# Projecting q and k from x before it is normalised, with GpSimd scaling h for the LRU and v

## The chip, the cores and the metric

The kernel runs on one core of a Trainium2 chip. The metric is the device time of one execution in microseconds, the median of several runs. Everything is float32; each weight matrix is read once from HBM, 1 MB at a time.

## The reference, cut to what matters

```python
h = rms_norm(x, mix_norm_g)                 # x: 256 tokens x 1024
proj = h @ w_in                             # 1024 x 2560
xr, yg, q, k, v = jnp.split(proj, splits, axis=-1)
xr = causal_depthwise_conv(xr, ...)
y_lru = rg_lru(xr, ...) * gelu(yg)
q = rms_norm(q.reshape(.., HEADS, HEAD_DIM), q_norm_g)   # 8 heads of 64
k = rms_norm(k.reshape(.., HEADS, HEAD_DIM), k_norm_g)
y_attn = moba_attention(q, k, v)            # causal attention over one block of 256
x = x + concat(rms_norm(y_lru), rms_norm(y_attn)) @ w_out
hf = rms_norm(x, ffn_norm_g)
up = causal_depthwise_conv(hf @ w_up, ...)  # 1024 x 5632
gate, val = jnp.split(up, 2, axis=-1)
x = x + (gelu(gate) * val) @ w_down         # 2816 x 1024
```

`rms_norm(x, g)` is `x * rsqrt(mean(x*x) + 1e-6) * g` over the last axis. As q and k are normalised again in each head, a factor that is the same for a whole token cancels there, but for the 1e-6: with x instead of the normalised x, the head's root needs 1e-6 * (mean(x*x) + 1e-6) in its place.

## The kernel before, in words

Each float32 product is made of three products of a rounded type: an operand is split in a high part (the value rounded) and a low part (the value less the high part), and high x high, high x low and low x high are added in PSUM (`three`, lines 953 to 959).

**The stream of weights.** The weights come as units of 128 x 1024, two units to a transfer `raw[n]` of 1 MB, six transfers in flight, in the order of their use: units 0 to 3 are w_in's columns of q, 4 to 7 k, 8 to 11 the LRU's input, 12 to 15 its gate branch, 16 to 19 v, 20 to 27 w_out, then the FFN's. SyncE issues the two halves of x (128 tokens each, lines 268 and 269), then unit 0 (line 272), unit 1 (line 273), `raw[1]` to `raw[5]` (line 275), and from then on a transfer whenever VectorE has finished with a buffer. ScalarE copies a unit's high part to a ring of six (`hi(u)`, line 336), VectorE makes its low part (`lo(u)`, line 627), and TensorE waits for `lo_done` before it uses the unit. Unit 0 is split by halves, the first half by VectorE alone (lines 669 and 664), the second half's high part by ScalarE (line 376).

**The start.** TensorE does 14 products of a matrix of ones (`warm_up(WARM_UP)`, line 1008). ScalarE and VectorE meanwhile sum the squares of x (lines 347, 361, 651), take the root and the reciprocal (358, 365, 641) and scale x to `x_norm` (354, 645), for the first 128 tokens and then the second. TensorE transposes `x_norm` (line 1014: eight transposes for each half); ScalarE reads each chunk of 128 channels from PSUM, times the gain, into h's high part (`h_part`, line 370), and VectorE makes its low part (line 659).

**Up to the attention.** TensorE's list (from line 1058) is: q's units 0 to 3 (`rows_unit`, 12 products each, tokens in PSUM's rows), k's 4 to 7, the LRU's 8 and 9 (`cols_unit`, channels in the rows, 24 products each), the transposes of q and k (line 1020), which wait for `qk_norm` (line 1064), units 10 and 11 with the scores of the first heads between them, and so on. For the q and k norms ScalarE squares an accumulator (line 392), VectorE sums it by heads (690), ScalarE takes the root (396), VectorE the reciprocal (695) and the scaling (697). Each engine works through its list in order, which is written out by hand. ScalarE's and VectorE's lists have `hi` and `lo` of a unit at fixed places: h_part(0), unit 0's half, h_part(1), h_part(2), unit 1, h_part(3 to 5), unit 2, h_part(6), h_part(7), units 3 to 8, the q norms, units 9 to 11, the k norms, units 12 and 13.

GpSimd's list is short: constants, the parameters' transfer (line 306), the table of distances (lines 313 and 316), eight small fills, and, once VectorE has made unit 3's low part (`lo_done` 4), the transfer of the LRU's gate weights (line 326). It computes nothing after that.

The tiles `decay` and `gate_i` hold `x_norm` at the start, and `tanh_a` a square; all are free until the LRU's gates.

Of the kernel before, what the change touches and what calls it, by code (L numbers as in the profile page):

```python
# [30 lines left out]
P = 128  # L31
D_MODEL = 1024
SEQ = 256
# [65 lines left out]
def build_layer(nc, x, stream, params, gates, out):  # L99
    with ExitStack() as ctx:  # L100
# [34 lines left out]
        small = sb("small", [P, 208])  # L135
# [19 lines left out]
        x_norm = [flat(decay), flat(gate_i)]  # L155
        sq_tok = flat(p_T)[:, 2560:3072]
# [12 lines left out]
        x_part, x_mean = small[:, 206:207], small[:, 207:208]  # L169
# [14 lines left out]
        warm, x_normed = sem("warm"), [sem(f"x_normed{m}") for m in range(TT)]  # L184
        first_hi, first_lo = sem("first_hi"), sem("first_lo")
        x_sq, x_sq_1 = sem("x_sq"), sem("x_sq_1")
        own_hi, q_scale_done, f_added = sem("own_hi"), sem("q_scale_done"), sem("f_added")
        x_rms_done, x_rec = sem("x_rms_done"), sem("x_rec")
# [41 lines left out]
        Q_ACC, K_ACC, X_ACC = bank[0:2], bank[2:4], bank[4:8]  # L230
        Y_ACC, V_ACC = bank[2:4], bank[4:6]
# [34 lines left out]
        def _(sp):  # L266
# [5 lines left out]
            sp.dma_start(raw[0][:, 0:UNIT], stream[0, :, 0:UNIT]).then_inc(first_landed, 16)  # L272
# [54 lines left out]


        @block.scalar
        def _(act):  # L330
# [11 lines left out]

            act.wait_ge(consts, 1)
            act.activation(warm_out, eps, ACT.Sqrt).then_inc(warm, 1)

            act.wait_ge(x_landed[0], 16)
            act.activation(flat(ygate), x_tok[:, 0, :], ACT.Square, accum_out=x_ss[:, 0:1]).then_inc(x_sq, 1)
            def x_root(m):
                act.activation(x_rms[:, m:m + 1], x_ss[:, m:m + 1], ACT.Sqrt, bias=eps,
                               scale=1.0 / D_MODEL).then_inc(x_rms_done, 1)  # L350

            def x_scale(m):
                act.wait_ge(x_rec, m + 1)
                act.activation(x_norm[m][:, 0:F_CUT], x_tok[:, m, 0:F_CUT], ACT.Copy,
                               scale=x_rstd[:, m:m + 1]).then_inc(x_normed[m], 1)

            act.wait_ge(x_sq, 1)
            act.activation(x_rms[:, 0:1], x_ss[:, 0:1], ACT.Sqrt, bias=eps, scale=1.0 / D_MODEL).then_inc(x_rms_done, 1)

            act.wait_ge(x_landed[1], 16)  # L360
            act.activation(flat(ygate)[:, 0:512], x_tok[:, 1, 512:1024], ACT.Square, accum_out=x_ss[:, 1:2]).then_inc(x_sq, 1)
            x_scale(0)
            act.wait_ge(x_sq, 2)
            act.wait_ge(x_sq_1, 1)
            act.activation(x_rms[:, 1:2], x_ss[:, 1:2], ACT.Sqrt, bias=x_mean, scale=1.0 / D_MODEL).then_inc(x_rms_done, 1)
            x_scale(1)

            def h_part(kc):
# [927 lines left out]
```

## Time and profile before

| | |
|---|---|
| median of 3 runs | 304.53 us (304.36 to 304.56) |
| the profiled execution | 304.15 us |
| its span | 302.4 us |
| TensorE busy | 295.6 us, 98% of the span |
| VectorE busy | 242.1 us, 80% |
| ScalarE busy | 200.7 us, 66% |
| GpSimd busy | 3.9 us, 1% |
| granted TensorE clock | 1.0 of full speed |

The profile is one execution. Its span runs from the first to the last instruction; the profiled execution's own time is 1.75 us longer. PE is TensorE, PEld its weight loads, ACT ScalarE, DVE VectorE, POOL GpSimd, SPq SyncE's queue. Busy time of an engine that is not the bottleneck may be free; an engine that is busy 98% sets the time wherever it does not wait.

### The profile page before, as it was taken

The numbers are of one execution on the slowest core, as the hardware profiler recorded it, in microseconds if no ns is written. First come the engines' busy times: TensorE is split into PE (matmuls) and PEld (weight loads), VectorE is DVE, ScalarE is ACT, GpSimd is POOL, SyncE is SP. The second block draws the span as 40 slices with busy tenths as digits, with TensorE's granted clock in tenths as the row PEclk, the third lists the DMA queues.
The fourth block names the chain that finished last, engine by engine and source line by source line (L and its number), as shares of the span: only waits on it lengthen the run. The fifth ranks groups of instructions, "written<-read, shape, count | busy, mean of one in ns | idle before, by whom it ended". The sixth has DMA issues, their size and how long they took to land.

```text
span 302.4 us, 4942 instructions
## 1 busy us (share of the span) xinstructions
PE 295.6 (98%) x1656; PEld 255.2 (84%) x1656; DVE 242.1 (80%) x432; ACT 200.7 (66%) x370; POOL 3.9 (1%) x21
## 2 busy tenths in 40 slices
PE   8999999999999999899999999999999999999995
PEld 8788998898988788788888888888888888888884
DVE  2998597798799767899878888887788888787764
ACT  6874598997756376887666667666666666766540
POOL 4000000000000000000000000000000000000000
PEclk9999999999999999999999999999999999999999
DMA  7999843034406701566554445373645545300003
GB/s 247 427 420 424 369 146 139 2 139 139 141 8 261 288 2 18 185 238 252 207 203 148 172 159 230 139 277 139 256 160 170 202 148 180 132 0 0 0 0 139
DMA packets 7983, 52.22 MB, mean 173 GB/s; under 512 B 896, under 2 KB 896, under 8 KB 2080
## 3 DMA queue, kind: packets, MB, share of 16 engines
q1 hardware_dynamic: 7776, 51.38, 45.5%
q0 software_dynamic: 192, 0.64, 0.6%
q8 instruction: 9, 0.15, 0.2%
q14 instruction: 6, 0.05, 0.1%
HBM read 50.98 MB, written 1.05 MB: 172 GB/s over the span
## 4 chain that ended last, share of the span: by engine, by line
PE 91%; DVE 3%; DMA 2%; ACT 1%; issue 1%; SPq 0%; ACTq 0%
PE bank L1201 27%; PE bank L955 15%; PE bank L956 15%; PE bank L959 15%; PE bank L1203 13%; DMA raw<-in_stream_dram 2%; PE bank L1031 1%; DVE x_tok L947 1%; PE bank L1044 1%; DVE w_lo L627 1%; PE bank L1150 1%; PE bank L1149 1%; PE bank L1020 1%; PE bank L1143 1%; PE bank L1051 1%
## 5 line engine op out<-in xcount | busy, mean ns | idle before, releaser
L1201 PE MATMUL bank<-h_both,w_hi 128*128 128x512 f32 x352 | 125.1, 398 | 1.5 <-DVE w_lo L627 1.2
L627 DVE TENSOR_TENSOR w_lo<-raw,w_hi 128x1024 fp32r<-128x1024 f32 x93 | 111.0, 1221 | 10.0 <-ACT w_hi L336 9.0
L1203 PE MATMUL bank<-h_both,w_lo 128*128 128x256 f32 x352 | 98.7, 280 | 0.0
L336 ACT ACTIVATE w_hi<-raw 128x1024 fp32r<-128x1024 f32 x87 | 88.9, 1053 | 6.1 <-PE bank L959 4.6
L1201 PEld LDWEIGHTS bank<-h_both,w_hi 128*128 128x128 f32 x352 | 66.1, 188 | 18.0 <-issue 2.0
L1203 PEld LDWEIGHTS bank<-h_both,w_lo 128*128 128x128 f32 x352 | 66.4, 189 | 0.7
L554 ACT ACTIVATE tanh_a<-bank 128x256 f32<-128x256 f32 x44 | 16.8, 382 | 45.9 <-PE bank L1203 45.9
L956 PE MATMUL bank<-w_lo,act_hi 128*128 128x512 f32 x88 | 34.5, 392 | 0.0
L955 PE MATMUL bank<-w_hi,act_hi 128*128 128x512 f32 x88 | 34.5, 392 | 0.0
L959 PE MATMUL bank<-w_hi,act_lo 128*128 128x512 f32 x88 | 34.2, 389 | 0.0
L885 DVE TENSOR_TENSOR ygate<-bank,tanh_a 128x256 f32<-128x256 f32 x44 | 18.5, 421 | 13.2 <-ACT tanh_a L554 13.2
L562 ACT ACTIVATE xc<-ygate,par 128x256 f32<-128x256 f32 x44 | 26.2, 595 | 2.0 <-DVE ygate L885 2.0
L896 DVE SCALAR_TENSOR_TENSOR xc<-ygate,par,xc 128x254 f32<-128x254 f32 x44 | 21.3, 483 | 5.1 <-DVE xc L892 0.2
L892 DVE SCALAR_TENSOR_TENSOR xc<-ygate,par,xc 128x255 f32<-128x255 f32 x44 | 21.1, 481 | 3.4 <-ACT xc L562 3.1
L955 PEld LDWEIGHTS bank<-w_hi,act_hi 128*128 128x128 f32 x88 | 16.5, 188 | 3.9
L959 PEld LDWEIGHTS bank<-w_hi,act_lo 128*128 128x128 f32 x88 | 16.5, 188 | 3.6
L955 PE MATMUL bank<-w_hi,h_both 128*128 128x512 f32 x48 | 19.0, 396 | 0.6 <-DVE h_both L659 0.6
L956 PEld LDWEIGHTS bank<-w_lo,act_hi 128*128 128x128 f32 x88 | 16.5, 188 | 2.7
L959 PE MATMUL bank<-w_hi,h_both 128*128 128x512 f32 x48 | 18.7, 390 | 0.0
L956 PE MATMUL bank<-w_lo,h_both 128*128 128x512 f32 x48 | 18.7, 389 | 0.0
L955 PE MATMUL bank<-h_both,w_hi 128*128 128x256 f32 x64 | 18.7, 292 | 0.0
L956 PE MATMUL bank<-h_both,w_hi 128*128 128x256 f32 x64 | 18.1, 283 | 0.0
(162 smaller groups left out, 388.3 us busy)
## 6 DMA issues: line engine op xcount, KB each, us to landing
raw<-in_stream_dram SPq DMA_DIRECT2D x46, 1024.0 KB, 4.8
x_tok<-in_x_dram SPq DMA_DIRECT2D x2, 512.0 KB, 3.7
raw<-in_stream_dram SPq DMA_DIRECT2D x2, 512.0 KB, 7.0
out_dram<-x_tok SPq DMA_DIRECT2D x4, 256.0 KB, 2.1
p_T<-in_gates_dram POOLq DMA_DIRECT2D x1, 512.0 KB, 8.7
par<-in_params_dram POOLq DMA_DIRECT2D x1, 117.0 KB, 4.9
```

Of the source, the lines that this page charges most:

```text
L336: act.activation(w_hi[u % RING][:, :], raw_unit(u), ACT.Copy).then_inc(hi_done, 1)
L554: act.activation(cross[which][s % 2], up_bank(s, which)[:, SEQ:2 * SEQ], ACT.Copy).then_inc(cross_out, 1)
L562: act.activation((conv_g, conv_v)[which][s % 2], joined[which][s % 2], ACT.Identity, bias=par[:, bass.ds(col + FFN_B, 1)], scale=par[:, ba ...
L627: dve.tensor_tensor(w_lo[u % RING][:, :], raw_unit(u), w_hi[u % RING][:, :].bitcast(F32), ALU.subtract).then_inc(lo_done, 1)
L885: dve.tensor_tensor(joined[which][s % 2], up_bank(s, which)[:, 0:SEQ], cross[which][s % 2], ALU.add).then_inc((joined_g, joined_v)[which], 1)
L892: dve.scalar_tensor_tensor(acc[:, 1:SEQ], joined[which][s % 2][:, 0:SEQ - 1], par[:, bass.ds(col + (FFN_W + 2 * STEPS), 1)], acc[:, 1:SEQ] ...
L896: dve.scalar_tensor_tensor(acc[:, 2:SEQ], joined[which][s % 2][:, 0:SEQ - 2], par[:, bass.ds(col + FFN_W, 1)], acc[:, 2:SEQ], ALU.mult, AL ...
L955: pe.matmul(acc, lhs_hi, rhs_hi, start=first, stop=False)
L956: pe.matmul(acc, lhs_hi, rhs_lo, start=False, stop=False)
L959: return pe.matmul(acc, lhs_lo, rhs_hi, start=False, stop=last)
L1201: pe.matmul(acc[:, :], whi[:, kc, :], h_both[:, kc, :, :].rearrange("p b t -> p (b t)"), start=kc == 0, stop=False)
L1203: ins = pe.matmul(acc[:, 0:SEQ], wlo[:, kc, :], h_hi[:, kc, :], start=False, stop=kc == KC - 1)
```

## The change

Three things are changed.

1. TensorE transposes x as it lands. `h_part` makes from it `q_hi` and `q_lo` (x times the gain, not normalised; they use the tiles `mix_hi` and `mix_lo`), and q's and k's units multiply those. The heads' roots get `qk_bias`, a number for each token, so that one root instruction becomes two (one for each 128 tokens).
2. The mean squares of x are summed by ScalarE alone, the first half at once, the second after h_part(7) and before `hi(3)`. VectorE makes the means (`x_mean_squares`) ahead of `lo(3)`, and after it the reciprocal roots and two diagonal matrices (`x_diagonals`). After unit 2, TensorE multiplies ones by the diagonals: each token's factor stands then in all rows of a bank, and ScalarE copies it to `x_rows` after `hi(5)`. GpSimd adds `q_hi` and `q_lo` (eight instructions of 128 x 256) and multiplies by `x_rows` (eight more) into `h_norm`, in the tiles `decay` and `tanh_a`. ScalarE and VectorE split `h_norm` in `h_hi` and `h_lo`, after the q norms and around unit 9. The LRU's, its gate branch's and v's units use those; unit 8 waits for them chunk by chunk (`hn_lo`).
3. The transfer of unit 0 is issued by ScalarE, ahead of its first instruction, and not by SyncE.

```diff
@@ sync
-            sp.dma_start(raw[0][:, 0:UNIT], stream[0, :, 0:UNIT]).then_inc(first_landed, 16)
@@ gpsimd
+            pool.wait_ge(dist_done, TT + HEADS)
+            pool.wait_ge(hT_lo, KC)
+            for kc in range(KC):
+                pool.tensor_tensor(h_norm[kc], q_hi[:, kc, :].bitcast(F32), q_lo[:, kc, :].bitcast(F32),
+                                   ALU.add).then_inc(h_joined, 1)
+            pool.wait_ge(x_rows_done, 1)
+            for kc in range(KC):
+                pool.wait_ge(h_joined, kc + 1)
+                pool.tensor_tensor(h_norm[kc], h_norm[kc], x_rows[:, :], ALU.mult).then_inc(h_normed, 1)
@@ scalar
+            act.dma_start(raw[0][:, 0:UNIT], stream[0, :, 0:UNIT]).then_inc(first_landed, 16)
...
-            (squares, roots and x_scale of both halves)
+            x_square(0)
...
             for kc in (6, 7):
                 h_part(kc)
-            his(3, 4, 5, 6, 7, 8)
+            x_square(1)
+            his(3)
+            act.wait_ge(x_ms_done, 1)
+            act.activation(x_rms, x_ms, ACT.Sqrt).then_inc(x_rms_done, 1)
+            his(4, 5)
+            act.wait_ge(x_spread, 1)
+            act.activation(x_rows[:, :], X_ROWS, ACT.Copy).then_inc(x_rows_done, 1)
+            his(6, 7, 8)
...
+            act.wait_ge(qk_bias_done, 1)
             roots(0)
-            his(9, 10, 11)
+            for kc in range(4):
+                h_norm_hi(kc)
+            his(9)
+            for kc in range(4, KC):
+                h_norm_hi(kc)
+            his(10, 11)
@@ vector
-            (reciprocals, squares and x_scale of both halves)
...
             for kc in (6, 7):
                 h_part(kc)
+            x_mean_squares()
             los(3)
+            x_diagonals()
...
             head_norms(0, Q_ACC)
-            los(9, 10, 11)
+            for kc in range(4):
+                h_norm_lo(kc)
+            los(9)
+            for kc in range(4, KC):
+                h_norm_lo(kc)
+            los(10, 11)
@@ tensor
             for m in range(TT):
-                pe.wait_ge(x_normed[m], 2)
+                pe.wait_ge(x_landed[m], 16)
                 for kc in range(KC):
-                    ins = pe.transpose(x_at(kc)[...], x_norm[m][:, P * kc:P * (kc + 1)], ident[:, :])
+                    ins = pe.transpose(x_at(kc)[...], x_tok[:, m, P * kc:P * (kc + 1)], ident[:, :])
...
             for j in range(4):
-                rows_unit(U_Q + j, U_Q, Q_ACC, hT_lo)
+                rows_unit(U_Q + j, U_Q, Q_ACC, q_hi, q_lo, hT_lo)
+                if j == 2:
+                    pe.wait_ge(x_diag, TT)
+                    for m in range(TT):
+                        ins = pe.matmul(X_ROWS[:, P * m:P * (m + 1)], ones[:, :], diag[:, m, :], start=True, stop=True)
+                    ins.then_inc(x_spread, 1)
             for j in range(4):
-                rows_unit(U_K + j, U_K, K_ACC)
-            cols_unit(U_X, X_ACC[0][:, 0:SEQ])
+                rows_unit(U_K + j, U_K, K_ACC, q_hi, q_lo)
+            cols_unit(U_X, X_ACC[0][:, 0:SEQ], h_ready=hn_lo)
```

The new functions, as far as they are not told above:

```python
def x_diagonals():                                    # VectorE
    dve.wait_ge(x_rms_done, 1)
    link(dve.reciprocal(x_rstd, x_rms))
    dve.wait_ge(consts, 2)
    for m in range(TT):
        dve.tensor_scalar(diag[:, m, :], ident[:, :], x_rstd[:, m:m + 1], None, ALU.mult).then_inc(x_diag, 1)

def h_norm_hi(kc):                                    # ScalarE
    act.wait_ge(h_normed, kc + 1)
    act.activation(h_hi[:, kc, :], h_norm[kc], ACT.Copy).then_inc(hn_hi, 1)

def h_norm_lo(kc):                                    # VectorE
    dve.wait_ge(hn_hi, kc + 1)
    dve.tensor_tensor(h_lo[:, kc, :], h_norm[kc], h_hi[:, kc, :].bitcast(F32), ALU.subtract).then_inc(hn_lo, 1)
```

## Rows read from the trace of the kernel before

**Rows 1.** The page, busy us (share of the span) xinstructions.

```profile
PE 295.6 (98%) x1656; PEld 255.2 (84%) x1656; DVE 242.1 (80%) x432; ACT 200.7 (66%) x370; POOL 3.9 (1%) x21
```

**Rows 2.** Chain of waits to the first weight product: start us, us, what.

```profile
1.75 6.20 DMA raw<-in_stream_dram
...
9.12 0.41 DVE h_both L659
...
9.67 0.47 PE bank L955
```

**Rows 3.** Timeline of TensorE's weight loads: start us, us, engine line op.

```profile
1.08 6.03 PEld L1005 LDWEIGHTS bank<-ones 128*128 128x128 f32 x28 [1.08 <-POOL ones L304]
7.14 0.86 PEld L1014 LDWEIGHTS bank<-ident,decay 128*128 128x128 f32 x8
7.96 0.91 PEld L1014 LDWEIGHTS bank<-ident,gate_i 128*128 128x128 f32 x8
```

**Rows 4.** Timeline of ScalarE from 4 to 17 us.

```profile
4.11 1.06 ACT L347 ACTIVATE ygate<-x_tok 128x1024 f32<-128x1024 f32 x1 [1.79 <-DMA x_tok<-in_x_dram]
...
5.29 0.29 ACT L358 ACTIVATE small<-small 128x1 f32<-128x1 f32 x1
...
8.44 0.47 ACT L370 ACTIVATE h_both<-bank,par 128x256 fp32r<-128x256 f32 x1 [0.64 <-PE bank L1014]
...
12.46 1.06 ACT L336 ACTIVATE w_hi<-raw 128x1024 fp32r<-128x1024 f32 x1 [0.27 <-DMA raw<-in_stream_dram]
...
14.14 2.95 ACT L336 ACTIVATE w_hi<-raw 128x1024 fp32r<-128x1024 f32 x3
```

**Rows 5.** Timeline of VectorE from 6 to 37 us.

```profile
6.48 0.54 DVE L645 TENSOR_SCALAR decay<-x_tok,small 128x640 f32<-128x640 f32 x1
...
11.14 1.23 DVE L627 TENSOR_TENSOR w_lo<-raw,w_hi 128x1024 fp32r<-128x1024 f32 x1 [0.20 <-ACT w_hi L336]
...
15.49 1.22 DVE L627 TENSOR_TENSOR w_lo<-raw,w_hi 128x1024 fp32r<-128x1024 f32 x1
...
16.75 5.76 DVE L627 TENSOR_TENSOR w_lo<-raw,w_hi 128x1024 fp32r<-128x1024 f32 x5
...
32.42 0.69 DVE L690 TENSOR_REDUCE small<-p_T 128x8 f32<-128x512 f32 x1 [2.54 <-ACT p_T L392]
...
35.18 1.29 DVE L697 TENSOR_TENSOR qk_tok<-bank,small 128x512 f32<-128x512 f32 x2
```

**Rows 6.** Timelines of TensorE: unit 3's first product, the q/k transposes, line 1114.

```profile
17.99 0.39 PE L955 MATMUL bank<-w_hi,h_both 128*128 128x512 f32 x1
...
37.35 1.91 PE L1020 MATMUL bank<-ident,qk_tok 128*128 128x128 f32 x16
...
82.58 0.66 PE L1114 MATMUL bank<-diag,ones 128*128 128x128 f32 x4
83.08 0.33 PE L1149 MATMUL bank<-v_tok,p_T 128*128 128x64 f32 x2
```

**Rows 7.** Groups of VectorE: xcount | busy us, mean ns | idle before.

```profile
L636 DVE TENSOR_SCALAR diag<-ident,small 128x128 f32<-128x128 f32 x2 | 0.6, 288 | 0.1
```

**Rows 8.** Timeline of GpSimd, 3 to 18 us.

```profile
3.56 0.40 POOL L316 TENSOR_SCALAR_AFFINE_SELECT neg_dist<-neg_dist 128x256 f32<-128x256 f32 x1
4.02 1.14 POOL L322 MEMSET small<- 64x1 f32 x8
17.01 0.59 POOL L326 DMA_DIRECT2D p_T<-in_gates_dram  x1 [11.85 <-DVE w_lo L627]
```

**Rows 9.** Groups of ScalarE and VectorE with SBUF operands of 128x256.

```profile
L574 ACT ACTIVATE act_hi<-gate_i 128x256 fp32r<-128x256 f32 x22 | 8.9, 403 | 1.4 <-DVE gate_i L905 1.4
L910 DVE TENSOR_TENSOR act_lo<-gate_i,act_hi 128x256 fp32r<-128x256 f32 x22 | 9.2, 419 | 0.5 <-ACT act_hi L574 0.5
```

**Rows 10.** DMA issues, KB each, median us from issue to landing.

```profile
x_tok<-in_x_dram SPq DMA_DIRECT2D x2, 512.0 KB, 3.7
raw<-in_stream_dram SPq DMA_DIRECT2D x2, 512.0 KB, 7.0
```

More of the change, by code:

```diff
@@ L155, in build_layer @@
         x_norm = [flat(decay), flat(gate_i)]
+        q_hi, q_lo = mix_hi, mix_lo
+        h_norm = [(decay, tanh_a)[kc // LC][:, kc % LC, :] for kc in range(KC)]
         sq_tok = flat(p_T)[:, 2560:3072]
@@ L183, in build_layer @@
         dist_done = sem("dist_done")
-        warm, x_normed = sem("warm"), [sem(f"x_normed{m}") for m in range(TT)]
+        warm = sem("warm")
+        x_ms_done, qk_bias_done, x_diag, x_spread, x_rows_done = (
+            sem("x_ms_done"), sem("qk_bias_done"), sem("x_diag"), sem("x_spread"), sem("x_rows_done"))
+        h_joined, h_normed, hn_hi, hn_lo = sem("h_joined"), sem("h_normed"), sem("hn_hi"), sem("hn_lo")
         first_hi, first_lo = sem("first_hi"), sem("first_lo")
-        x_sq, x_sq_1 = sem("x_sq"), sem("x_sq_1")
+        x_sq = sem("x_sq")
         own_hi, q_scale_done, f_added = sem("own_hi"), sem("q_scale_done"), sem("f_added")
-        x_rms_done, x_rec = sem("x_rms_done"), sem("x_rec")
+        x_rms_done = sem("x_rms_done")
         xT, hT_hi, hT_lo = sem("xT"), sem("hT_hi"), sem("hT_lo")
@@ L230, in build_layer @@
         Q_ACC, K_ACC, X_ACC = bank[0:2], bank[2:4], bank[4:8]
+        X_ROWS = bank[6][:, 0:SEQ]
         Y_ACC, V_ACC = bank[2:4], bank[4:6]
@@ new lines, in x_diagonals @@
+            def x_diagonals():
+                dve.wait_ge(x_rms_done, 1)
+                link(dve.reciprocal(x_rstd, x_rms))
+                dve.wait_ge(consts, 2)
+                for m in range(TT):
+                    dve.tensor_scalar(diag[:, m, :], ident[:, :], x_rstd[:, m:m + 1], None, ALU.mult).then_inc(x_diag, 1)
+            def h_norm_lo(kc):
+                dve.wait_ge(hn_hi, kc + 1)
+                dve.tensor_tensor(h_lo[:, kc, :], h_norm[kc], h_hi[:, kc, :].bitcast(F32),
+                                  ALU.subtract).then_inc(hn_lo, 1)
@@ L657, in h_part @@
             def h_part(kc):
                 dve.wait_ge(hT_hi, kc + 1 if kc < 4 else kc + 2 - kc % 2)
-                dve.scalar_tensor_tensor(h_lo[:, kc, :], x_at(kc), par[:, MIX_G + kc:MIX_G + kc + 1],
-                                         h_hi[:, kc, :].bitcast(F32), ALU.mult, ALU.subtract).then_inc(hT_lo, 1)
+                dve.scalar_tensor_tensor(q_lo[:, kc, :], x_at(kc), par[:, MIX_G + kc:MIX_G + kc + 1],
+                                         q_hi[:, kc, :].bitcast(F32), ALU.mult, ALU.subtract).then_inc(hT_lo, 1)
@@ L989, in rows_unit @@
                         tok = slice(P * m, P * (m + 1))
-                        ins = three(banks[m][:, :], h_hi[:, kc, tok], h_lo[:, kc, tok],
+                        ins = three(banks[m][:, :], lhs_hi[:, kc, tok], lhs_lo[:, kc, tok],
                                     w_hi[u % RING][:, cols], w_lo[u % RING][:, cols], kc == 0, kc == KC - 1)
```

68 lines of the change are left out of this document (23 added, 45 removed).

## The prediction

> **What bounds the kernel now.** I read the page's busy times first: TensorE is busy 98% of the span [rows 1], so only time in which it waits, or products added to it, can move the end. The span is 302.4 us, the profiled execution 304.15 us (1.75 us around the span), the median of the runs 304.53 us. I work in differences on the span and add them to the median.
>
> The chain of waits at the start says what the first weight product waits for [rows 2]: the transfer of unit 0 (landed 7.95), what VectorE makes of it, then h's low part, and the product at 9.67. That reads as if weights and normalisation were both too late. The second view to read is the timeline of the engine at the end of that chain [rows 3]: TensorE's 14 warm-up products end at 7.11 and the transposes of x follow at 7.14 and 7.96 without a gap. x_norm[0] was ready at 7.02 (VectorE's share, 6.48 + 0.54 [rows 5]), so the warm-up, not the normalisation, releases the transposes. The third view is ScalarE's own timeline [rows 4]: from 8.44 it works without a gap until 12.19 and then waits 0.27 us for raw[1], whose two units are units 2 and 3. VectorE behind it makes unit 1's low part at 11.14 to 12.37 [rows 5], and TensorE starts unit 1 right then. So units 1 to 3 are paced by ScalarE's list and by raw[1] landing at about 12.42, after which TensorE runs without a gap: unit 3 starts at 17.99, the q/k transposes at 37.35 [rows 6].
>
> **The change part by part.**
>
> *No normalisation before the transposes.* Removed: about 2.5 us of ScalarE and 1.9 us of VectorE work between 5.3 and 7.8. All of it lay beside the warm-up products, whose count the diff leaves at 14. The transposes start at 7.14 as before and h_part(0) on ScalarE at 8.44 as before. Gain: 0 on this path; the most it could be is the 0.09 us between 7.02 and 7.11. x must now have landed by 7.14 and 7.96. x took a median 3.7 us from issue [rows 10] and ScalarE began on the first half at 4.11 [rows 4], so the second came near 5.4; cover 2.5 us or more.
>
> *First weights through ScalarE's queue.* They are issued at about 0.83 instead of 1.75. Both x halves then share the transfer engines with them. All three transfers were through by 7.95 [rows 2], in whatever order, and that is the worst for x's second half; midway between 5.4 and 7.95 is 6.7. Its transposes start at 7.96 [rows 3]: covered. ScalarE's issue (0.4 us) and its table load end before x lands at 4.11. Gain: the first half's cast and subtraction are no longer in front of h_lo(0), which waited for VectorE until 9.04. It could start at 8.44 + 0.47 + 0.03 = 8.94, so the first product comes 0.1 us earlier. Unit 1 still needs VectorE's subtraction at 11.14, which waited for ScalarE's copy [rows 5], and that copy's place behind h_part(2) is the same: the 0.1 us is given back at 12.4. If the issue stood behind the table load, at 2.1 us, all would be 0.35 us late. Neither end reaches unit 3 by more than that; I take 0.
>
> *The square of x's second half, moved.* It now stands on ScalarE between h_part(7) and hi(3). Before, hi(3) started at 14.14. The full square costs 1.18 us, start to next start (4.11 to 5.29 [rows 4]). hi(3) starts at 15.3 and ends at 16.37; VectorE's lo(3) runs 16.41 to 17.63 where it had started at 15.49 (+0.92). TensorE would have needed lo(3) at 17.99: covered by 0.36 us.
>
> *The new row products.* TensorE now waits after unit 2 for two diagonals that VectorE makes behind lo(3): a reciprocal (0.16 us and its wait) and two scalings of 0.29 us that overlap to about 0.5 [rows 7], done at 18.25 to 18.3. Unit 3's products, which need nothing of this, are queued behind: wait 0.3 us. The two f32 products cost 0.50 us, as the same pair at line 1114 shows (82.58 to 83.08 [rows 6]). Unit 3 starts at 18.8: **+0.8 us**. Ends: +0.4 if raw[1] lands 0.3 us or more earlier, since then only the products remain; +1.3 if the extra queue makes it land 0.5 us later.
>
> *GpSimd joins and scales h.* Its list has the gates' transfer ahead, which waited for lo(3) and was issued at 17.01, 0.59 us long [rows 8]; with lo(3) 0.92 us later, the first sum starts at about 18.3, not when q_lo is there at 15.6. Then 8 sums and 8 scalings of 128x256. No row shows GpSimd with two operands. One operand of this size took 0.40 us: lower end. Two read one after the other, 0.80 us: upper end. I take 0.6, nearer the row: 16 x 0.6 = 9.6, done at 27.9. By the Trainium skill (GPSIMD Engine Reference, Performance versus the Vector engine) 4497 ns for 2048 elements gives an estimate of about 0.6 us too. Unit 8 starts at 31.6 + 0.8 and takes the chunks one by one; ScalarE's eight copies (0.40 [rows 9]) have to follow. Cost 0 for TensorE up to about 0.75 us an instruction.
>
> *VectorE's list grows.* Added before the k norms, in start-to-start times: lo(3) late 0.92; reciprocal and diagonals 0.6; a second square root in the q round 0.2; eight low parts of h at 0.42 us less 0.08 overlap [rows 9], 2.7. Together 4.4 us. The head sums of k began at 32.42 after 2.54 us of idle time [rows 5], so lo(11) had ended at 29.88; it now ends at 34.3 and they begin 1.9 us later. With one more square root the k norms, which ended at 35.18 + 1.29 = 36.47, end at 38.5, and TensorE arrives at 37.35 + 0.8 = 38.15: **a new wait of 0.4 us** (0 if the 0.08 overlaps are larger; 1 if VectorE loses 0.6 us more).
>
> Sum: +0.8 + 0.4 = +1.2 us. Behind line 1064 TensorE is gapless again until long after, so nothing is given back: 304.15 + 1.2 = 305.35 for the profiled execution, and against the median **305.7 us** (own range 304.9 to 306.5).
>
> **The rivals.**
>
> *Port: VectorE and GpSimd hold each other up (+7.2, 311.7 us).* From 18.3 on, VectorE's list is subtractions of two SBUF operands of 1.22 us (five in a row from 16.75 [rows 5]) and the eight short ones, and GpSimd's 16 instructions lie beside them. If each must wait for the other's to end and they take turns, VectorE waits behind four of its five long subtractions and six of the following ones, ten times 0.6 = 6.0 us; it has no slack left, so TensorE gets all of it before the q/k transposes: 1.2 + 6.0. With 0.4 us it is 309.7, with 0.8 313.7. It decides as soon as VectorE loses over 0.4 us. For it: a VectorE without idle time in this stretch. Against it: nothing in this trace, since GpSimd computes only until 5.2 us [rows 8], when VectorE has no such instruction; no row bears on it.
> The Trainium skill (SBUF — State Buffer, Who interferes with whom) states exactly this mechanism: a VectorE instruction with two SBUF inputs contends with a GpSimd instruction that reads SBUF, whoever is first holding the ports for the whole instruction. By that rule this rival is the result; no run here shows it yet.
>
> *GpSimd is slow alone (+3.6, 308.1 us).* At 0.9 us an instruction, 16 x 0.15 us past the cover of 0.75 is 2.4 us more. For it: a two-operand form that no row shows. Against: 0.40 us for one operand.
>
> *Not slower (+0.4, 304.9 us, within the measurement).* raw[1] lands before 12.1, because the queue of x gives up 512 KB or a lower rate of the first transfers fills up. Then ScalarE's copy of unit 2 starts at 12.19, the diagonals are ready when unit 2 ends, and the k norms are just in time; left are 0.5 us of row products less 0.1 at the start. For it: the first weights took 6.2 us from issue [rows 2] and the 512 KB loads a median 7.0 [rows 10]. Against it: all bytes ahead of raw[1] are the same.
>
> *Faster (303.8 us).* If the warm-up's end is only modelled late and the transposes start at 6.7, with the stream 1 us earlier too, units 1 to 3 come 0.4 us or more earlier and outweigh the products. Against it: rows 3 show no gap.
>
> **How the numbers follow.** Forecast 0.40, port 0.27, GpSimd slow 0.08, not slower 0.17, faster 0.08. A measurement of this kernel tells about 0.2%, 0.6 us, from no change. Slower: 0.37 of the forecast's 0.40 plus 0.35, 0.72; same: 0.03 + 0.17, 0.20; faster 0.08. The range 304.2 to 312.2 leaves out the faster case and the port case with the longest instructions. The signs hold different weights, so the forecast's own range stands above.
>
> **What would show it.** First transposes at 7.1 and unit 1 at 12.4 as before (else the first two parts are wrong); a wait of TensorE for the diagonals and unit 3 near 18.8; subtractions of line 627 still 1.22 us apart by 1.14 beside GpSimd (the port rival stretches them or opens gaps to about 1.8); GpSimd done by 28; k norms near 38.5. A VectorE gap or stretch of over 0.5 us per instruction after 18.3 would make 305.7 wrong upward; raw[1] landing before 12.1, downward.

## The result and the profile after

The changed kernel takes 311.07 us (median of 4 runs, 310.95 to 312.63) against 304.5 us before; the ratio is 1.0228, 95% interval 1.0196 to 1.0261. That is slower by 6.6 us where 305.7 was forecast, and 0.6 us below the 311.7 that the port rival gave. The profiled execution took 310.95 us, its span is 309.2 us against 302.4. Executions more than 1.5% above the fastest of their kernel are left out of the times and ratios below: three of seven of the kernel with the results scaled (312.77 to 314.32 us, mean granted clock 0.978 to 0.984) and one of 12 of the kernel without GpSimd's work and with the queue back (593 us).

Busy time, from the page of the kernel after (columns as in [rows 1]):

```profile
PE 298.4 (96%) x1660; PEld 256.9 (83%) x1660; DVE 247.6 (80%) x438; ACT 202.8 (66%) x378; POOL 21.9 (7%) x37
```

GpSimd's 16 new instructions are 18.0 us of that, 1.1 us each, where the forecast had 0.6. TensorE has only four instructions more, but it waits. The waits of TensorE, us in total, times, longest:

```profile
PE bank L982 <- DVE h_both L674: 2.0, 2, 1.8
PE bank L1047 <- DVE qk_tok L719: 2.0, 1, 2.0
...
PE bank L1041 <- DMA x_tok<-in_x_dram: 0.3, 1, 0.3
```

The timeline of TensorE says where the loss arises. Shown are the transposes of x, the first product, unit 1, the row products, unit 3, unit 8's first and fifth chunk, and the q/k transposes:

```profile
6.84 1.04 PE L1041 MATMUL bank<-ident,x_tok 128*128 128x128 f32 x8
8.15 1.09 PE L1041 MATMUL bank<-ident,x_tok 128*128 128x128 f32 x8 [0.28 <-DMA x_tok<-in_x_dram]
9.72 0.47 PE L982 MATMUL bank<-w_hi,mix_hi 128*128 128x512 f32 x1 [0.48 <-DVE mix_lo L679]
...
12.57 0.50 PE L982 MATMUL bank<-w_hi,mix_hi 128*128 128x512 f32 x1
...
18.17 0.60 PE L1090 MATMUL bank<-diag,ones 128*128 128x128 f32 x4
18.53 0.48 PE L982 MATMUL bank<-w_hi,mix_hi 128*128 128x512 f32 x1
...
32.22 0.28 PE L982 MATMUL bank<-h_both,w_hi 128*128 128x256 f32 x1
...
35.60 0.39 PE L982 MATMUL bank<-h_both,w_hi 128*128 128x256 f32 x1 [1.78 <-DVE h_both L674]
...
44.12 1.09 PE L1047 MATMUL bank<-ident,qk_tok 128*128 128x128 f32 x8 [1.96 <-DVE qk_tok L719]
```

Up to unit 3 the change costs 0.54 us (18.53 against 17.99 [rows 6]). The q/k transposes start at 44.12 against 37.35 [rows 6]: 6.77 us, which is all of the loss (6.8 us on the span). Behind them nothing comes and nothing is given back. So the question is what made the k norms, the last thing the transposes wait for, end at 44.07 instead of 36.47 [rows 5]. Timeline of VectorE:

```profile
17.91 7.40 DVE L647 TENSOR_TENSOR w_lo<-raw,w_hi 128x1024 fp32r<-128x1024 f32 x5
...
30.57 0.68 DVE L674 TENSOR_TENSOR h_both<-decay,h_both 128x256 fp32r<-128x256 f32 x1 [0.20 <-ACT h_both L370]
...
37.56 2.36 DVE L647 TENSOR_TENSOR w_lo<-raw,w_hi 128x1024 fp32r<-128x1024 f32 x2 [0.48 <-ACT w_hi L352]
39.84 0.68 DVE L712 TENSOR_REDUCE small<-p_T 128x8 f32<-128x512 f32 x1
...
42.78 1.29 DVE L719 TENSOR_TENSOR qk_tok<-bank,small 128x512 f32<-128x512 f32 x2
```

The five subtractions in a row took 5.76 us before [rows 5] and take 7.40 now: VectorE lost 1.6 us there. Behind 30 us it has gaps, and they end with ScalarE. Timeline of ScalarE, the last copies of h and what stands behind them:

```profile
29.42 0.42 ACT L370 ACTIVATE h_both<-decay 128x256 fp32r<-128x256 f32 x1 [1.52 <-POOL decay L342]
...
35.30 0.42 ACT L370 ACTIVATE h_both<-tanh_a 128x256 fp32r<-128x256 f32 x1 [1.25 <-POOL tanh_a L342]
36.16 0.42 ACT L370 ACTIVATE h_both<-tanh_a 128x256 fp32r<-128x256 f32 x1 [0.45 <-POOL tanh_a L342]
36.49 1.99 ACT L352 ACTIVATE w_hi<-raw 128x1024 fp32r<-128x1024 f32 x2
```

And timeline of GpSimd, the new instructions in their four groups of four:

```profile
18.24 7.67 POOL L337 TENSOR_TENSOR decay<-mix_hi,mix_lo 128x256 f32<-128x256 f32 x4
25.87 2.82 POOL L337 TENSOR_TENSOR tanh_a<-mix_hi,mix_lo 128x256 f32<-128x256 f32 x4
28.65 3.19 POOL L342 TENSOR_TENSOR decay<-decay,x_rows 128x256 f32<-128x256 f32 x4
31.80 4.33 POOL L342 TENSOR_TENSOR tanh_a<-tanh_a,x_rows 128x256 f32<-128x256 f32 x4
```

The second group is the measure of GpSimd undisturbed: 2.82 us for four, 0.70 from start to start and 0.74 long each, while VectorE reduces p_T (one operand, in SBUF) and begins to scale q out of PSUM. The first group, beside the five subtractions, takes 7.67. The chain then reads: the end of GpSimd's last scaling (36.13), ScalarE's copy (36.16), the high parts of units 10 and 11 queued behind it (36.49), VectorE's low parts (37.56), the squares and sums of k (39.84), the roots, the k norms (44.07).

The turn-taking itself is seen in two single instructions. First VectorE, then GpSimd, from windows between 22.5 and 25 us:

```profile
21.87 1.76 DVE L647 TENSOR_TENSOR w_lo<-raw,w_hi 128x1024 fp32r<-128x1024 f32 x1
...
23.55 1.76 DVE L647 TENSOR_TENSOR w_lo<-raw,w_hi 128x1024 fp32r<-128x1024 f32 x1
```

```profile
22.51 1.72 POOL L337 TENSOR_TENSOR decay<-mix_hi,mix_lo 128x256 f32<-128x256 f32 x1
```

The first of these subtractions ends at 23.63. GpSimd's sum, issued at 22.51, ends 0.60 behind that, at 24.23, and the next subtraction ends 1.1 behind that. These times fit two engines of which neither is interrupted and the one that comes second waits for the whole of the other. A turn takes 1.68 us (1.14 + 0.54), so VectorE loses 0.54 per turn and GpSimd about 1.0. The turns begin late, though. The first sum, issued at 18.24, let two subtractions pass and took 2.63 us:

```profile
18.24 2.63 POOL L337 TENSOR_TENSOR decay<-mix_hi,mix_lo 128x256 f32<-128x256 f32 x1
```

Those first two subtractions were not stretched (1.22 us each), so VectorE lost three times 0.54, the 1.6 us.

One more thing stands between 37 and 41 us. The row of windows 38 to 39 us (PE busy, PEld, DVE, ACT, POOL, granted clock, DMA share, GB/s):

```profile
38.00:39.00 1.00, 1.00 (x7) 1.00 (x6) 1.00 (x2) 0.96 (x2) 0.00 (x0) 0.50 0.97 410
```

After the 1.78 us wait in unit 8 the granted clock is 0.50 (1.2 GHz) from 37.1 to 40.5 and the products are 0.21 apart instead of 0.12. Here that is hidden: the k norms end 2 us later still.

### The profile page after: what moved, and what is told of

It is laid out like the page before. It is cut to its first block, busy times and chain, and to the rows that moved or that the text cites. A ratio compares the mean times of both kernels' runs of the same rounds, so it can differ in the third digit from the quotient of the medians.

```text
span 309.2 us, 4984 instructions
## 1 busy us (share of the span) xinstructions
PE 298.4 (96%) x1660; PEld 256.9 (83%) x1660; DVE 247.6 (80%) x438; ACT 202.8 (66%) x378; POOL 21.9 (7%) x37
## 4 chain that ended last, share of the span: by engine, by line
PE 81%; issue 5%; POOL 5%; DVE 5%; ACT 2%; POOLq 0%; ACTq 0%
PE bank L1233 26%; PE bank L1235 13%; PE bank L982 12%; PE bank L983 12%; PE bank L986 12%; POOL decay L337 2%; PE bank L1058 1%; DVE w_lo L647 1%; POOL tanh_a L337 1%; DVE x_tok L974 1%; ACT p_T L533 1%; PE bank L1071 1%; DVE h_both L887 1%; POOL decay L342 1%; ACT w_hi L352 1%
## 5 line engine op out<-in xcount | busy, mean ns | idle before, releaser
L647 DVE TENSOR_TENSOR w_lo<-raw,w_hi 128x1024 fp32r<-128x1024 f32 x93 | 112.9, 1240 | 10.3 <-ACT w_hi L352 9.5
L1235 PE MATMUL bank<-h_both,w_lo 128*128 128x256 f32 x352 | 98.7, 280 | 0.0
L982 PE MATMUL bank<-w_hi,mix_hi 128*128 128x512 f32 (+1 forms) x72 | 26.9, 374 | 0.5 <-DVE mix_lo L679 0.5
L986 PE MATMUL bank<-w_hi,mix_lo 128*128 128x512 f32 (+1 forms) x72 | 26.4, 366 | 0.0
L983 PE MATMUL bank<-w_lo,mix_hi 128*128 128x512 f32 (+1 forms) x72 | 26.4, 366 | 0.0
L982 PE MATMUL bank<-h_both,w_hi 128*128 128x256 f32 x64 | 19.5, 305 | 2.0 <-DVE h_both L674 2.0
L986 PE MATMUL bank<-h_both,w_lo 128*128 128x256 f32 x64 | 18.8, 294 | 0.0
L983 PE MATMUL bank<-h_both,w_hi 128*128 128x256 f32 x64 | 18.8, 294 | 0.0
```

What stands on the lines that cost most here:

```text
L647: dve.tensor_tensor(w_lo[u % RING][:, :], raw_unit(u), w_hi[u % RING][:, :].bitcast(F32), ALU.subtract).then_inc(lo_done, 1)
L982: pe.matmul(acc, lhs_hi, rhs_hi, start=first, stop=False)
L983: pe.matmul(acc, lhs_hi, rhs_lo, start=False, stop=False)
L986: return pe.matmul(acc, lhs_lo, rhs_hi, start=False, stop=last)
L1235: ins = pe.matmul(acc[:, 0:SEQ], wlo[:, kc, :], h_hi[:, kc, :], start=False, stop=kc == KC - 1)
```

## The experiments

Two theories were put against each other. **Lateness:** TensorE loses because GpSimd's list ends late and the h chain stands in front of the k norms. **VectorE's loss:** TensorE loses what the subtractions lose. The kernel before was run again beside each, on the same chip. Its median was 304.62 us beside the kernel without GpSimd's work, the one with long fills, the one with one operand on GpSimd and the one with the traffic beside the kernel before; 304.98 us beside the ones with one operand on VectorE, with half the instructions, with the queue back in the kernel after and with the results scaled; and 304.87 us beside the other four.

### GpSimd's work taken out

```
-  pool.tensor_tensor(h_norm[kc], q_hi, q_lo, ALU.add) ... pool.tensor_tensor(h_norm[kc], h_norm[kc], x_rows, ALU.mult)
   h_norm_hi(kc):  act.activation(h_hi, q_hi, ACT.Copy)         # was h_norm[kc], with a wait for GpSimd
   h_norm_lo(kc):  dve.tensor_tensor(h_lo, q_hi, h_hi, ALU.subtract)
```

> The changed kernel without GpSimd's 16 instructions; ScalarE and VectorE split q_hi instead of the scaled h (so the LRU and v get a wrong factor; the work of all other engines is unchanged). Port theory (the two engines hold each other up at SBUF): line 647's five subtractions after unit 3 go back from 7.40 to 5.8 us, the k norms end near 38.5 instead of 44.07, time 305.0 to 305.7. GpSimd-is-slow theory: the same, since it leaves GpSimd out. If the loss came from something else (the row products, the longer lists of ScalarE and VectorE), the time stays above 308.

Measured: 305.09 us (305.07 to 305.21), ratio 1.0003 [0.9958, 1.0048]. VectorE's timeline:

```profile
18.08 5.76 DVE L639 TENSOR_TENSOR w_lo<-raw,w_hi 128x1024 fp32r<-128x1024 f32 x5
...
36.99 1.29 DVE L711 TENSOR_TENSOR qk_tok<-bank,small 128x512 f32<-128x512 f32 x2
```

Everything else of the change is still in (only the scaling of h is left out): the transposes of raw x, the squares moved, the diagonals, the row products, 16 more short instructions on ScalarE and VectorE, the queue. All that costs 0.5 us or less; GpSimd's 16 instructions cost 6.0.

### GpSimd busy, but only writing

```
-  pool.tensor_tensor(h_norm[kc], ...)                      # 16 of them
+  pool.memset(flat(decay if kc % 2 else tanh_a), 0.0)      # 16 fills of 128x1024, then of 128x656
```

Both read h as in the experiment above and keep all waits for GpSimd. First with 1024 columns:

> As the kernel without GpSimd's work, but GpSimd does 16 fills of 128x1024 in its place, which read nothing, and ScalarE's eight copies wait for the last eight. Port theory, with reading as what collides: GpSimd's fills keep one duration whether VectorE subtracts or not, line 647 stays at 1.14 us from start to start; the time is that of the kernel without GpSimd if a fill is under 0.75 us, more by 16 times the excess. Any-GpSimd-work theory: fills and subtractions stretch each other as in the changed kernel, over 308.

Then with 656 columns:

> As the kernel with 16 fills in place of GpSimd's sums and scalings (h is not scaled), but each fill of 656 columns instead of 1024, so about 0.64 us each and 0.70 apart: the pace of undisturbed two-operand instructions. Theory (lateness of GpSimd's list is the whole price; at this pace unit 8's cover hides it): GpSimd ends near 29.6 to 30.2, the k norms end near 38.3 to 38.8, and the time is 305.1 us (304.9 to 305.8), as without GpSimd. Rival (anything that puts the h chain in the lists behind GpSimd costs the k norms, whatever its pace): the k norms end near 40 and the time is 307 or more.

Measured: 310.74 us (310.59 to 310.78), ratio 1.0187 [1.0141, 1.0233], with 1024 columns, and 305.04 us (304.85 to 305.21), ratio 1.0010 [1.0001, 1.0019], with 656. The last fill of each, GpSimd's timeline, and of the kernel with the shorter ones VectorE's:

```profile
33.47 0.95 POOL L341 MEMSET decay<- 128x1024 f32 x1
```

```profile
28.83 0.65 POOL L341 MEMSET decay<- 128x656 f32 x1
```

```profile
17.96 5.76 DVE L647 TENSOR_TENSOR w_lo<-raw,w_hi 128x1024 fp32r<-128x1024 f32 x5
...
36.86 1.29 DVE L719 TENSOR_TENSOR qk_tok<-bank,small 128x512 f32<-128x512 f32 x2
```

Fills aren't held up, and hold nobody up: 1.01 and 0.70 us apart throughout, VectorE's five at 5.76. So here lateness stands alone. The long fills end at 34.42 and the k norms at 42.36; the short ones, at the pace of undisturbed two-operand instructions, end at 29.48 and cost nothing. That is the lateness theory with VectorE's loss excluded. The forecast's cover, by which GpSimd's instructions cost TensorE nothing up to 0.75 us each, is confirmed too: 16 x (1.01 - 0.75) = 4.2 us, and the k norms moved from 38.15 to 42.36.

The time moved by 5.7, not 4.2. TensorE's q/k transposes show the rest:

```profile
42.42 3.36 PE L1047 MATMUL bank<-ident,qk_tok 128*128 128x128 f32 x16 [3.54 <-DVE qk_tok L719]
```

The granted clock fell to 0.50 in that wait of 3.54 us, at 41.9, and stayed there until 45.3; the 16 transposes took 3.36 instead of 1.91 us [rows 6].

### What GpSimd reads

```
-  pool.tensor_tensor(h_norm[kc], q_hi, q_lo, ALU.add)      /  pool.tensor_tensor(h_norm[kc], h_norm[kc], x_rows, ALU.mult)
+  pool.tensor_scalar(h_norm[kc], q_hi, 1.0, None, ALU.mult) /  pool.tensor_scalar(h_norm[kc], h_norm[kc], 1.0, None, ALU.mult)
```

> The changed kernel with each of GpSimd's 16 instructions reading one operand of 128x256 (a product with 1.0) in place of two. Port theory: still stretched beside VectorE's subtractions, though GpSimd alone takes about 0.4: the five subtractions take 6.5 to 7.4 us, time 306 to 309. GpSimd-is-slow theory (two operands are slow on GpSimd itself): each takes 0.4 throughout, subtractions back to 5.8 us, time as without GpSimd, about 305.5.

Measured: 312.13 us (311.97 to 313.29), ratio 1.0241 [1.0192, 1.0290]. Timeline of GpSimd, first and second group, and of VectorE:

```profile
18.48 6.75 POOL L337 TENSOR_SCALAR decay<-mix_hi 128x256 f32<-128x256 f32 x4
25.20 3.29 POOL L337 TENSOR_SCALAR tanh_a<-mix_hi 128x256 f32<-128x256 f32 x4
```

```profile
18.15 6.37 DVE L646 TENSOR_TENSOR w_lo<-raw,w_hi 128x1024 fp32r<-128x1024 f32 x5
```

One operand less doesn't help. Such an instruction is held off as well (6.75 us for four), and undisturbed they are 0.82 us apart, more than the two-operand one's 0.70. Both theories had put it at 0.4 us, so both missed the time (306 to 309 and 305.5). VectorE was stretched too, but less: 6.37 us for its five, against 7.40 beside two-operand sums and 5.76 alone. So both forms of a reading GpSimd instruction take part, and the fills, which read nothing, don't.

### What VectorE reads

```
   lo(u):
+      if u in (4, 5, 6, 7, 8):
+          dve.tensor_scalar(w_lo, raw_unit(u), 2.0 ** -13, None, ALU.mult); return
```

> The kernel after, with VectorE's subtractions of units 4 to 8 replaced by a scaling of raw alone (one SBUF operand, same output tile; the low parts of these units are then not the right ones). GpSimd's 16 two-operand instructions stay. Theory (what holds GpSimd off is that VectorE reads two SBUF operands, not that it is busy): GpSimd's sums take 0.74 us from the first, all 16 end at 29.6 to 30.5 instead of 36.1, the k norms end near 38.5 and the time is 305.0 to 305.6 us. Rival (any VectorE instruction that reads SBUF holds it off while it runs): the sums take 0.9 to 1.5 us, GpSimd ends at 32 or later and the time is over 307.

Measured: 310.05 us (308.53 to 311.08), ratio 1.0174 [1.0136, 1.0211]. Timeline of GpSimd and, second, VectorE:

```profile
17.68 1.74 POOL L332 DMA_DIRECT2D p_T<-in_gates_dram  x1 [12.48 <-DVE w_lo L650]
19.49 3.73 POOL L337 TENSOR_TENSOR decay<-mix_hi,mix_lo 128x256 f32<-128x256 f32 x4
...
23.19 1.19 POOL L337 TENSOR_TENSOR tanh_a<-mix_hi,mix_lo 128x256 f32<-128x256 f32 x1
```

```profile
18.01 1.29 DVE L648 TENSOR_SCALAR w_lo<-raw 128x1024 fp32r<-128x1024 f32 x2
20.30 3.48 DVE L648 TENSOR_SCALAR w_lo<-raw 128x1024 fp32r<-128x1024 f32 x3 [1.00 <-ACT w_hi L352]
...
40.41 1.29 DVE L722 TENSOR_TENSOR qk_tok<-bank,small 128x512 f32<-128x512 f32 x2
```

The theory fell. The rival holds for this instruction: the sums that met a scaling took 1.19 us, the three scalings from 20.30 took 3.48 us where two alone take 1.29, and even the issue of the gates' transfer took 1.74 instead of 0.59 [rows 8], until the two scalings at 18.01 were through. It doesn't hold for any VectorE instruction that reads SBUF, as the expectation put it: in the kernel after the sum of p_T over the heads, which reads 128x512 from SBUF, ran from 26.63 to 27.32 beside sums of 0.74 us. The scalings are shorter, so GpSimd ended at 33.75, not 36.13, and the k norms at 41.70, not 44.07: the same 2.4 us. What was wrong in the expectation is that it freed GpSimd: 30.5 at the latest. That the issue of a transfer is held up is read from one row only, and it is not the whole of the same mechanism: in the kernel after the same issue began at 17.58 and met a subtraction at 17.91, 0.33 us later as here, and took 0.59.

### The same traffic beside the kernel before

```
   # kernel before
+  for n in range(16):
+      pool.tensor_tensor(scratch, neg_dist[:, 0:SEQ], neg_dist[:, P:P + SEQ], ALU.add)   # nobody waits for it
+      pool.wait_ge(loads_done, n + 1)
```

> The kernel before, with 16 GpSimd sums of 128x256 added behind the gates' transfer (from about 17.6 us), for which no engine waits. Port theory: the five subtractions from 16.75 take about 7.4 us instead of 5.76, the sums take about 1.9 us beside them and 0.7 when VectorE is idle; TensorE loses at most 0.3 us, since VectorE had 2.5 us of idle time before the k norms: 304.5 to 304.9. GpSimd-is-slow theory: subtractions as before, sums of one length, 304.5.

Measured: 305.11 us (304.60 to 305.30), ratio 1.0000 [0.9954, 1.0046]. The first sum, GpSimd's timeline, and the five subtractions beside it, VectorE's:

```profile
18.18 5.44 POOL L331 TENSOR_TENSOR scratch<-neg_dist 128x256 f32<-128x256 f32 x1
```

```profile
17.25 5.77 DVE L633 TENSOR_TENSOR w_lo<-raw,w_hi 128x1024 fp32r<-128x1024 f32 x5
...
26.89 4.57 DVE L633 TENSOR_TENSOR w_lo<-raw,w_hi 128x1024 fp32r<-128x1024 f32 x3
```

With nobody waiting for GpSimd the traffic costs TensorE nothing that can be measured, though the later subtractions are stretched as in the kernel after (4.57 us for three, against 3.49 in the kernel before, from 26.39). The five in a row were not, where 7.4 us was expected: GpSimd's first sum stood through all of them, 5.44 us, and VectorE lost nothing. In the kernel after the first sum stood through two of them and then the two engines alternated. Who gets the next turn is thus not fixed; why the first sum got none here is open. The sums here read other tiles and each waits for the one before it, and neither was tried alone.

### Half the instructions

```
-  8 sums, then 8 scalings of the sum
+  8 x pool.tensor_tensor(h_norm[kc], q_hi, x_rows, ALU.mult)
```

> The kernel after with GpSimd's eight sums left out, so that it scales the high part of h alone: eight two-operand instructions instead of 16. Theory (one GpSimd instruction gets through per VectorE subtraction, 1.7 us apart, and what counts is when the list ends): it starts at 19.2 when x_rows is there, gets four through until VectorE's subtractions end at 25.3, the rest at 0.74, and ends near 28.5, ahead of what the copies of h need; the k norms end at 38.3 to 39 and the time is 305.1 to 306.0 us. VectorE still loses 1.0 to 1.6 us in its five subtractions, which are then seen not to matter. Rival (what VectorE loses is what TensorE loses): the k norms end 1 to 1.6 us later than without GpSimd, at 39.3 to 39.9, and the time is 306.1 to 306.7.

Measured: 306.65 us (306.46 to 306.86), ratio 1.0054 [1.0038, 1.0070]. VectorE's timeline:

```profile
17.87 7.40 DVE L643 TENSOR_TENSOR w_lo<-raw,w_hi 128x1024 fp32r<-128x1024 f32 x5
...
38.42 1.29 DVE L715 TENSOR_TENSOR qk_tok<-bank,small 128x512 f32<-128x512 f32 x2
```

GpSimd ended at 28.65 as expected, in good time. The k norms still ended at 39.71, 1.6 us later than with the short fills, and that is the 1.6 us that the five subtractions lost (7.40 against 5.76): here the rival theory is the right one, and it is what my rival in the prediction described. Both mechanisms exist. With GpSimd in time TensorE pays VectorE's loss, 1.6; with 16 instructions GpSimd's lateness is the longer path and covers it.

### The order of the lists

```
   his(9, 10, 11)                     # ahead of the eight h_norm_hi instead of between and behind them
   for kc in range(KC): h_norm_hi(kc)
   # and los(9, 10, 11) ahead of the eight h_norm_lo
```

> The kernel after, with the high and low parts of units 9, 10 and 11 put ahead of ScalarE's copies and VectorE's subtractions of h; GpSimd's 16 instructions stay. Theory (GpSimd's instructions are held to one per VectorE subtraction, and the k norms are late because they stand behind the h chain in both lists): hi(9..11) no longer wait for GpSimd, so the k norms wait only for eight subtractions of h behind GpSimd's end at about 36; they end near 41.2 instead of 44.1 and the time is about 308.2 us. Rival (the k norms are late because VectorE and TensorE themselves are slowed by GpSimd's traffic, whatever the order): 311 us as the kernel after. A second rival, that the order is right and the h part is needed early by unit 8: unit 8 waits over 3 us and the time is above 311.

Measured: 311.10 us (310.42 to 311.53), ratio 1.0203 [1.0183, 1.0222]: no change, and my 308.2 missed. TensorE's timeline at unit 8, and GpSimd's last group:

```profile
35.56 0.55 PE L976 MATMUL bank<-h_both,w_hi 128*128 128x256 f32 x1 [3.15 <-DVE h_both L671]
```

```profile
33.44 4.30 POOL L342 TENSOR_TENSOR tanh_a<-tanh_a,x_rows 128x256 f32<-128x256 f32 x4
```

Two things were left out of the expectation. The three subtractions now lie beside GpSimd's scalings, so its list ends at 37.74, 1.6 us later. And the first low part of h comes behind them: unit 8 waits 3.15 us, and the granted clock is 0.50 from 35.3 to 42.1 us. The second rival that the expectation named came true, as far as the wait goes. The k norms ended at 43.50, and TensorE reached the q/k transposes later still, at 44.62, without a wait. Order moves the wait from one place to the other; it doesn't remove it.

### The queue of the first weights

Alone on the kernel before, where x is normalised ahead of the transposes:

```
-  sp.dma_start(raw[0][:, 0:UNIT], ...)
+  act.dma_start(raw[0][:, 0:UNIT], ...)
```

> The kernel before, with only unit 0's transfer issued by ScalarE instead of SyncE. Theory (x then lands at about 8.2 instead of 5.4, and here x is normalised before it is transposed): x_norm[1] near 10.1, the first product near 11.6 instead of 9.7, about 1.9 us that TensorE can't give back: 306.5 us. Rival (the sixteen engines' rate is shared but x is small, or the warm-up hides it): first product within 0.3 of 9.7 and 304.5 us.

Taken back in the kernel after, and in the one without GpSimd's work:

> The kernel after with unit 0's transfer back on SyncE's queue. Theory (the start of the kernel lies ahead of GpSimd's lateness, which sets the k norms by itself): x lands 2 us earlier, the transposes of x no longer wait, the q/k transposes stay at 44.1 and the time is 311.0 us (310.8 to 311.5). Rival (the first units set GpSimd's start, so the loss moves with them): the time is 310.5 or less, or 311.7 or more where the first weights land later.

> The kernel without GpSimd's sums and scalings (h is not scaled), with unit 0's transfer back on SyncE's queue. Theory (x lands 2.3 us later through the second queue, and of that only some 0.2 to 0.3 us reaches TensorE, where the transposes wait for x): the wait for x goes, unit 3 starts 0.2 to 0.3 us earlier, and the time is 304.8 us against 305.1. Rival (the queue gives the stream an earlier first unit, which is what keeps this kernel so near the one before): the first product comes later than 9.9 and the time is 305.3 or more.

Measured: alone 307.51 us (307.41 to 308.67), ratio 1.0102 [1.0083, 1.0120]; taken back in the kernel after 312.96 us (311.50 to 313.86), ratio 1.0267 [1.0228, 1.0306]; taken back without GpSimd 305.42 us (304.75 to 307.15), ratio 1.0019 [0.9998, 1.0039]. TensorE's transposes in the first of them, then the first product in the second:

```profile
9.63 1.37 PE L1014 MATMUL bank<-ident,decay 128*128 128x128 f32 x8 [2.43 <-DVE decay L645]
```

```profile
10.76 0.47 PE L982 MATMUL bank<-w_hi,mix_hi 128*128 128x512 f32 x1 [1.78 <-DVE mix_lo L679]
```

The move has two sides. x takes 6.0 us from issue to landing instead of 3.7 [rows 10]; where x must be squared, rooted and scaled first, the transposes wait 2.43 us, the granted clock is 0.50 from 10.3 to 13.7 us, and the kernel loses 2.6 us (I had expected 2). The changed kernel doesn't have that step in front and waits 0.3 us. On the other side unit 0 landed by 6.5 us in every profile with the move in which VectorE stood waiting for it (6.25 in the kernel after), and without the move at 8.8 to 9.1 in three profiles and at 7.95 in that of the kernel before, whose first product at 9.67 [rows 2] is thus an early one. With unit 0 late, lo(3) ends 0.6 us later, GpSimd starts at 18.82 instead of 18.24 and the k norms end at 44.66 instead of 44.07. So the start is not hidden behind GpSimd, as my theory had it; it is the start of GpSimd's path. The two profiled executions, both at a mean clock of 0.994, are 0.55 us apart (311.50 and 310.95); the rest of the 1.9 us between the medians goes with a lower clock, 0.989 in two of the four executions. In the kernel without GpSimd the difference is within what can be told; the 304.8 us that the theory expected was not reached, and the first product came at 10.47, as its rival had it.

### The scaling put on the results

```
   q_hi, q_lo = h_hi, h_lo                                   # one split of h for all units, never scaled
+  dve.tensor_tensor(X_ACC[c], X_ACC[c], x_rows, ALU.mult)   # 4, in PSUM; and 4 halves of Y_ACC
   act.activation(v_tok[:, m, :], V_ACC[m], ACT.Copy, scale=x_rstd[:, m])
```

> The change without GpSimd: h is not scaled at all; VectorE scales the accumulators of X and Y by x_rows in PSUM, and ScalarE's copy of V takes 1/rms as its scale, so the whole result is computed. Theory (TensorE pays only the four row products, 0.4 to 0.5 us, and the six scalings of 128x256, about 0.4 us each, lie beside it): k norms end near 37 and the time is 304.9 to 305.2 us, no faster than before, since the transposes of x start when the warm-up ends in either. Rival (the scalings stand between the convolution and what TensorE next waits for): 306 us or more. Second rival (with eight subtractions of h gone, units and norms come early enough that it beats the kernel before): 304.2 or less.

Measured: 307.93 us (307.88 to 308.07 in four executions), ratio 1.0094 [1.0059, 1.0130]. Waits of TensorE:

```profile
PE bank L1177 <- ACT v_tok L498: 1.3, 1, 1.3
...
PE bank L1080 <- DVE xc L729: 1.0, 1, 1.0
```

The k norms end at 37.35, earlier than in any other version of the change, and the price comes later: TensorE waits 1.0 us for the convolution, in front of which the scalings now stand in VectorE's list, and 1.3 for v's copy. Which of these each scaling causes was not separated. (The profile is of an execution of 314.32 us, whose granted clock was 0.50 from 84.0 to 97.7 us; only what lies before that is read from it, the wait for v's copy at 82.4 us as the last.) The first rival was right, and my 304.9 to 305.2 missed. No version beat the kernel before.

## Why the prediction was right and wrong

**One rule ties the runs.** In five kernels the k norms end 7.9 us after GpSimd's last instruction, whatever made that late:

| kernel | GpSimd ends | k norms end | difference | median us |
|---|---|---|---|---|
| short fills | 29.48 | 38.15 | 8.67, not bound | 305.04 |
| eight instructions | 28.65 | 39.71 | 11.06, VectorE's loss | 306.65 |
| one operand on VectorE | 33.75 | 41.70 | 7.95 | 310.05 |
| long fills | 34.42 | 42.36 | 7.94 | 310.74 |
| after | 36.13 | 44.07 | 7.94 | 311.07 |
| one operand on GpSimd | 35.99 | 43.92 | 7.93 | 312.13 |
| after, queue back | 36.72 | 44.66 | 7.94 | 312.96 |

GpSimd has to end by 38.15 - 7.94 = 30.2. Undisturbed its 16 instructions would have ended at 29.5 (the short fills). The first group lost 4.8 us (7.67 against 2.82), the scalings 1.8 (31.80 + 4.33 - 28.65 against two groups of 2.82), together 6.6; less the 0.7 that was to spare (30.2 - 29.5), 5.9, which is 44.07 - 38.15. With 0.5 for the row products that makes 6.4 of the 6.6 us between the medians. The two kernels at the foot of the table also lost time to the clock: their profiled executions had a mean of 0.989 and 0.994, and all eight of their executions were at 0.995 or below.

*Point by point.*

- *The front gains 0:* held. First transposes 6.84, first product 9.72, unit 1 12.57 against 9.67 [rows 2] and 12.4. It held against this profile of the kernel before, which is an early one: with the same start and GpSimd's traffic beside it the first product came at 10.61 (unit 0 landed at 8.9), 0.9 us later than in the kernel after. x's second half landed at about 8.1, not 6.7, and was not quite covered (0.28 us); it did not reach unit 1.
- *The square of x moved:* held but for its time. It ran at 13.87 already, and lo(3) started at 16.05, +0.56 instead of +0.92, since raw[1] was there when ScalarE asked (12.21, where it waited until 12.46 before [rows 4]). That is the "not slower" rival's mechanism, worth 0.25 us.
- *A wait of 0.3 for the diagonals:* did not come, mostly because of that.
- *Row products 0.5:* 0.36 to the next product, unit 3 +0.54 in all, where +0.8 was forecast.
- *GpSimd's instructions at 0.6, cost 0 up to 0.75:* **this is the step that failed.** Undisturbed 0.70 was near, and the cover of 0.75 was exact. But "no row bears on it" was taken as a reason to cost the contact with VectorE at nothing. Beside the subtractions an instruction measured 1.9 us in the first group, and the 16 ended at 36.13 where 27.9 was forecast.
- *The k norms 0.4 late:* 38.15 to 38.28 without contact, against a forecast of 38.5; with it 44.07.
- *The port rival (+7.2, measured +6.6):* its mechanism, turns of whole instructions, is shown, and its price per turn (0.6) too, at 0.54. Its path was not: it had VectorE lose ten turns. VectorE lost about three in its five subtractions, 1.6 us in all, and without GpSimd being late that is what TensorE would pay (the experiment with eight instructions). What bound was the other side of the lock, GpSimd's 6.6 us, passed on through ScalarE's and VectorE's lists. The size agreed partly by chance.

- *The forecast and the range:* 305.7 and its own range, 304.9 to 306.5, missed. The stated range, 304.2 to 312.2, holds the measured time because it was drawn round the rivals; that this range held is owed to the port rival's price, not to the forecast. Slower was forecast and came, but of the 6.6 us the forecast's own causes gave about 0.5 (305.09 without GpSimd's work, against 304.62).

The Trainium skill (SBUF — State Buffer, Who interferes with whom) says that a VectorE instruction with two SBUF inputs and a GpSimd instruction that reads SBUF contend, the first one holding the ports for its whole length; this case's trace agrees (1.76 and 1.72 us, 1.68 apart, against 1.22 and 0.74), but for the first sum, which began beside one subtraction and let a second pass. The same section lets a one-operand scaling on VectorE contend as well, where it runs in a mode that uses two ports. The run with one operand on VectorE agrees as far as it can be read: 1.19 us for a sum beside a scaling that reads raw alone, and scalings 0.60 us apart where the subtractions are 1.14; that they ran in such a mode no run here shows.

The chance was misjudged more than the mechanism: 0.27 for a collision that this page states, with a list of VectorE that has no idle time in the stretch and 16 instructions that all read SBUF, was low.

## What to carry to other kernels

GpSimd wasn't a free engine here beside a VectorE that works from SBUF. Count each of its SBUF-reading instructions as one VectorE instruction plus itself (1.7 us here for 0.7), and try them beside other work of VectorE: beside the sums over p_T and the scalings of q out of PSUM they ran at full pace. Then ask what stands behind it in the in-order lists: the work that GpSimd was given was not needed until 32 us, but the copies that waited for it stood ahead of the k norms, and so its lateness was TensorE's. And when a change removes a step from the front, look whether that step or something beside it (here the 14 warm-up products) was what the path waited for.

## What the runs showed of the hardware that was not expected

- GpSimd products of 128x256 with one SBUF operand came 0.82 us apart, the two-operand instructions 0.70.
- Of two engines that contend, one can be passed over several times: a sum of 0.74 us stood for 5.44 us beside five subtractions that took 5.77, and in the kernel after the first sum stood for 2.63 us.
- A VectorE scaling with one SBUF operand of 128x1024 held GpSimd up as well (1.19 instead of 0.74 us), and even the issue of a transfer (1.74 instead of 0.59 us, one row), which the subtractions didn't.
- GpSimd's fills neither lost nor took time (0.95 us each, VectorE's five at 5.76).
- In the profiles of eight kernels the granted clock fell to 0.50 (1.2 GHz) in a wait of TensorE of 1.3 to 3.5 us or within 1.6 us of its end and stayed there for 3.4 to 13.7 us. Other such waits had no such drop: 1.96 us in the kernel after, 1.69 with half the instructions. In the profile with one operand on VectorE a wait of 3.1 us had none either; of that kernel's four executions this one, at mean clock 0.999, took 308.53 us, and the others, at 0.989 to 0.994, 310.0 to 311.1. So in that kernel the lower clock goes with 1.5 to 2.5 us more; that the same wait caused it there is not shown, since only one execution has a trace.
- A transfer of 512 KB on a second queue made the two of x land in a median of 6.0 us instead of 3.7, and itself landed 1.5 us or more earlier than in the profiles without it.
